# The end of a fused transformer layer: order of the last gate/up and down products, the engine of the last norms, and the last store

## The chip, the cores and the metric

The kernel runs on the 8 cores of one Trainium2 chip. Each core works alone on its own share of the tokens; no data passes between cores. A core has five engines that run at the same time, each with a queue of its own that it works off in order: TensorE (PE, matrix products into PSUM), VectorE (DVE), ScalarE (ACT), GpSimd (POOL), and SyncE (SP), which here only issues transfers. The metric is the device time of the slowest core, in microseconds.

## The reference

One layer of a diffusion transformer over 2 sequences of 8192 latent tokens of width 1024, with 256 context tokens. What matters here is its second half:

```
h     = modulate(layer_norm(x), shift, scale)
mix   = token_mixer(h, ...)           # window attention + gated spatial mixing
x_mid = layer_norm(ALPHA * x + g1 * mix, ln1_g, ln1_b)
h2    = modulate(layer_norm(x_mid), shift2, scale2)
gate, up = split(h2 @ w_ffn_in)       # 2 x 2816 columns
y     = (silu(gate) * up) @ w_ffn_out # 2816 -> 1024
out   = layer_norm(ALPHA * x_mid + g2 * y, ln2_g, ln2_b)
```

The layer norm takes mean and variance over the 1024 columns of a token, subtracts the mean, multiplies by the inverse root of variance plus epsilon, and then by a gain and adds a bias, both of 1024 columns.

## The kernel before, in words

A core has 2048 tokens: 16 tiles of 128 tokens, in four groups of four tiles. Tokens lie on the partitions in the residual stream (`xm`, 128 x 1024 in float32 for a tile) and the model's columns lie on the partitions in the inputs of the matrix products (`hT`).

The hidden width of 2816 is cut into 11 rounds of 256 hidden columns. Rounds 0 to 6 run one after the other over all tiles: gate and up products (`gu`, L1160), SiLU of the gate on ScalarE (L1175), product of the two on VectorE (L1178), down products (`dn`), and the sum into `xm` on VectorE (L1209). The last four rounds (7 to 10, called late) run tile by tile: `late_gu` makes the gate and up products of a few tiles for all four rounds, and `late_dn` the down products of one tile over all four rounds in one go, 8 matmuls of 512 columns for each half of the 1024 output columns. All 8 must wait for the products of all four rounds: the waits stand ahead of the first of them. After a tile's two halves are summed, `final` (L1212) does its layer norm and its store.

A unit of `late_gu` is one of 2 x 4 (half of a round's columns, round) and has a gate part and an up part of 8 matmuls each. For groups 0 to 2 a unit covers four tiles (512 columns a matmul); for the last group it is cut into tiles 12 and 13, and tiles 14 and 15 (256 columns a matmul).

The norm in `final`: `stat` (L486) takes statistics of each half of 512 columns on VectorE (L493), joins them into mean and variance (L496), adds epsilon (L498), and GpSimd raises the sum to the power of minus one half (L500). For tiles 0 to 11 and tile 15, VectorE then does two instructions of 1024 columns: subtract the mean and multiply by the gain (L1222), then multiply by the inverse root and add the bias (L1224). For tiles 12, 13 and 14 the work is spread: VectorE makes the negative mean times the inverse root (L516), ScalarE normalizes (L1217), VectorE multiplies by the gain (L1219), and GpSimd adds the bias (L1220). Then SyncE issues a store of 128 x 1024 (L1226).

`stat` also serves the first norm (16 tiles, the halo and the context), the norm inside the gated spatial mixing, and `residual`, which makes `x_mid` from the mixer's output and then normalizes it again for `h2`.

The order on each engine's queue isn't the program's order. Each operation is given to a planner (`Plan`) with its engine, a due time (`prio`), an estimated cost, and what it comes `after`. `arrange` plays the program through once, before it is emitted: it takes, engine by engine, the operations that could start within a small slack of the earliest one, and of these the one with the lowest due time; buffers (PSUM banks, statistics slots) are dealt out in this order too. The gate and up parts draw on PSUM banks 0 to 3 (`MU`), the down products on banks 4 to 7 (`DU`). Operations that free a bank (L1175, L1178, L1209) have a due time 150 earlier than their products. What this yields is a fixed order for each engine, and the waits between them are semaphores. Operations listed as `behind` another only keep its place in the order and wait for nothing.

The due times of the end of the program, with `base` = 950:

```
late_gu(8, 4, base + 185, 10)
late_dn(4, 4, base + 193, 20)
late_gu(12, 2, base + 285, 5)
late_dn(8, 4, base + 293, 20)
late_gu(14, 2, base + 325, 5)
late_dn(12, 4, base + 375, 10)
```

The third number is the due time of the first unit or tile and the fourth the step to the next.

Of the kernel before, what the change touches and what calls it, by code (L numbers as in the profile page):

```python
# [9 lines left out]
ALU = mybir.AluOpType  # L10
# [4 lines left out]
NT = 16  # L15
# [7 lines left out]
EPS = 1e-5  # L23
# [287 lines left out]
def build_nc():  # L311
# [169 lines left out]

    def stat(prio, srcs, n, after, eps):

        w = len(srcs)  # L486
        st = Tile([tuple(('st', i + x) for x in range(w)) for i in range(0, 12, w)])
        m = 6 * n // 512
        b = []
        for i, src in enumerate(srcs):  # L490
            def f(e, i=i, src=src):
                for h in range(n // 512):
                    ins = e.bn_stats(out=stt[:, sid(st) + i, 6 * h:6 * h + 6], in_=src()[:, 512 * h:512 * h + 512])  # L493
                return ins
            a = P.op('dve', prio, 0.68 * n / 512, f, after=after[i], takes=[st] if i == 0 else [])
            b.append(P.op('dve', prio - 40, 0.21, lambda e, i=i: e.bn_aggr(  # L496
                out=mv[:, sid(st) + i, 0:2], in_=stt[:, sid(st) + i, 0:m]), after=[a]))
        v = P.op('dve', prio - 40, 0.17, lambda e: e.tensor_scalar(  # L498
            out=mv[:, sid(st):sid(st) + w, 4], in0=mv[:, sid(st):sid(st) + w, 1], scalar1=eps, scalar2=None, op0=ALU.add), after=b)
        r = P.op('pool', prio - 40, 0.75, lambda e: e.tensor_tensor(  # L500
            out=mv[:, sid(st):sid(st) + w, 2], in0=mv[:, sid(st):sid(st) + w, 4], in1=neghalf[:, 0:w], op=ALU.pow),
            after=[v, ms_nh])
        return r, st

    def mean_of(st, i=0):
# [538 lines left out]
    def residual(g, base, step, psb, tb, ld_ln):  # L1044
        tiles = []
        for i in range(4):
            t = 4 * g + i
            prio = base + step * i - i
            xs = xm[g][:, i, :]
            ld = P.dma('sp', prio + i, 512, lambda e, xs=xs, t=t: e.dma_start(out=xs, in_=xh[(t + 1) * 128:(t + 2) * 128, :]),  # L1050
                       'xm%d' % t, after=xm_free[g])
            rs = []
            for h in range(2):
                ps = banks(*psb)

                def f(e, ps=ps, h=h, i=i):
                    for k in range(8):
                        ins = e.matmul(bank(ps), lhsT=mg[g][:, k, i * 128:(i + 1) * 128], rhs=woutb[:, k, h * 512:(h + 1) * 512],  # L1058
                                       start=(k == 0), stop=(k == 7))
                    return ins  # L1060
                mm = P.op('pe', prio + i, 1.73, f, after=[t_mg[(m, g)] for m in range(8)] + t_wo, behind=xm_free[g], takes=[ps])
                wo_done[(t, h)] = mm
                rs.append(P.op('dve', prio + i - 150, 0.75, lambda e, ps=ps, h=h, xs=xs: e.scalar_tensor_tensor(
                    out=xs[:, h * 512:(h + 1) * 512], in0=xs[:, h * 512:(h + 1) * 512], scalar=2.0 * ALPHA, in1=bank(ps),
                    op0=ALU.mult, op1=ALU.add), after=[mm, ld], gives=[ps]))
            r, st = stat(prio + i, [lambda xs=xs: xs], 1024, [rs], 4 * EPS)
            a = P.op('dve', prio + i, 1.3, lambda e, xs=xs, st=st: e.scalar_tensor_tensor(
                out=xs, in0=xs, scalar=mean_of(st), in1=ln_v[:, 0], op0=ALU.subtract, op1=ALU.mult), after=[r, ld_ln])
            b = P.op('dve', prio + i, 1.3, lambda e, xs=xs, st=st: e.scalar_tensor_tensor(
                out=xs, in0=xs, scalar=rstd_of(st), in1=ln_v[:, 1], op0=ALU.mult, op1=ALU.add), after=[a], gives=[st])  # L1070
            t_xm[t] = b
            r, st = stat(prio + i, [lambda xs=xs: xs], 1024, [[b]], EPS)
            m = minus(st, prio + i, r)
            xb = slot('xb', 0, 1)
            xbv = lambda xb=xb: V(o_xn + 2 * KB * sid(xb), BF16, 1024)
            n = P.op('act', prio + i, 1.24, lambda e, xs=xs, st=st, xbv=xbv: e.activation(
                out=xbv(), in_=xs, func=AF.Identity, scale=rstd_of(st), bias=minus_of(st)),
                after=[m, att_done], behind=[xb_last[-1]] if xb_last else [], takes=[xb], gives=[st])
            xb_last.append(n)
            tiles.append((n, xb, xbv))  # L1080
            if i % 2 == 0:
                continue
            pair = tiles[-2:]
            cut = slice(g * 512 + (i - 1) * 128, g * 512 + (i + 1) * 128)
            for c4 in range(2):
                ps = banks(*tb)

                def f(e, ps=ps, pair=pair, c4=c4):
                    b = bankb(ps)
                    for ci in range(4):  # L1090
                        c = 4 * c4 + ci
                        for x in range(2):
                            ins = e.transpose(b[:, ci * 256 + x * 128: ci * 256 + (x + 1) * 128],  # L1093
                                              pair[x][2]()[:, c * 128:(c + 1) * 128], ident)
                    return ins
                tr = P.op('pe', prio + i, 0.5, f, after=[p[0] for p in pair], takes=[ps], gives=[p[1] for p in pair])
                for ci in range(4):
                    c = 4 * c4 + ci
                    t_h2[(g, i // 2, c)] = P.op('act', prio + i, 0.57, lambda e, ps=ps, ci=ci, c=c, cut=cut: modulate_out(
                        e, 'act', hT[:, c, cut], bankb(ps)[:, ci * 256:(ci + 1) * 256], 4, 3, c, 0),  # L1100
                        after=[tr, modc_ready[(3, c)], modc_ready[(4, c)]] + [h_done[(m_, g)] for m_ in range(8)], gives=[ps])
# [109 lines left out]

    def final(t, prio):  # L1212
        xs = xm[t // 4][:, t % 4, :]
        r, st = stat(prio, [lambda: xs], 1024, [[t_acc[(t, 0)], t_acc[(t, 1)]]], EPS)
        if t in (12, 13, 14):
            mi = minus(st, prio - 40, r)
            z = P.op('act', prio, 1.24, lambda e: e.activation(  # L1217
                out=xs, in_=xs, func=AF.Identity, scale=rstd_of(st), bias=minus_of(st)), after=[mi], gives=[st])
# [1 line left out]
            b = P.op('pool', prio, 2.4, lambda e: e.tensor_tensor(out=xs, in0=xs, in1=ln_v[:, 1], op=ALU.add), after=[a])  # L1220
        else:
            a = P.op('dve', prio, 1.3, lambda e: e.scalar_tensor_tensor(  # L1222
                out=xs, in0=xs, scalar=mean_of(st), in1=ln_v[:, 0], op0=ALU.subtract, op1=ALU.mult), after=[r, ld_ln2])
            b = P.op('dve', prio, 1.3, lambda e: e.scalar_tensor_tensor(  # L1224
                out=xs, in0=xs, scalar=rstd_of(st), in1=ln_v[:, 1], op0=ALU.mult, op1=ALU.add), after=[a], gives=[st])
        P.dma('sp', prio, 512, lambda e: e.dma_start(out=out_d[t * 128:(t + 1) * 128, :], in_=xs), 'out%d' % t, after=[b])  # L1226

    for r in range(NR):
# [39 lines left out]
    late_gu(8, 4, base + 185, 10)  # L1268
    late_dn(4, 4, base + 193, 20)
    late_gu(12, 2, base + 285, 5)  # L1270
    late_dn(8, 4, base + 293, 20)
    late_gu(14, 2, base + 325, 5)
    late_dn(12, 4, base + 375, 10)

    P.arrange()
    P.emit(nc, es)
# [142 lines left out]
```

How the kernel before makes its waits and increments, by code:

```python
            def body(engine, e=e):  # L269
                for o in self.q[e]:
                    for s, n in waits[o]:
                        engine.wait_ge(sems[s], n)
                    ins = o.fn(engine)
                    if o.tick is not None:
                        ins.then_inc(sems[o.tick[0]], 16 if o.key is not None else 1)
                if e == 'sp':
                    for k, n in sorted(final.items()):
                        engine.wait_ge(sems[k], n)
```

## Time and profile before

| what | us |
|---|---|
| median of 3 runs | 981.92 |
| lowest to highest | 981.34 to 982.61 |
| the profiled execution | 983.19 |
| its span, core 4, the slowest | 981.4 |
| spans of the eight cores | 975.6 to 981.4 |
| busy in the span: TensorE / VectorE / ScalarE / GpSimd | 897.0 / 624.9 / 321.6 / 275.3 |

The span goes from a core's first to its last instruction; the time of an execution also has what lies around it, 1.8 us here. Start times in the rows are microseconds from the start of the span on core 4. Matmuls are pipelined and their ends are modelled, so a long run of them is to be read by its whole length. Shares of busy time are averages over stages that have different limits, so they are read stage by stage. The granted clock of TensorE is a share of full speed.

### The profile page before, as it was taken

Reading aid. Unit: us, or ns where it says so; the run is one execution under the profiler, and the core shown is the slowest. Engines: PE = TensorE matmul, PEld = TensorE weight load, DVE = VectorE, ACT = ScalarE, POOL = GpSimd, SP = SyncE. Lnnn points to the kernel's source line nnn. Section 1 sums busy time; section 2 is a strip of 40 time slices with the busy share of each in tenths; the row PEclk is TensorE's granted clock in tenths of the full one; section 3 lists DMA queues with packets and bytes.
Section 4 is the critical chain, followed back from the end, with each engine's and each line's share of the span. In section 5 each row is a group of like instructions: output and inputs, shape, how many; then the busy total and the mean of one; then the engine's idle time right before and its main releaser. Section 6 shows DMA issues by size and latency. Waiting matters only on the chain.

```text
span 981.4 us, 15835 instructions; the slowest of 8 cores (975.6 to 981.4 us)
## 1 busy us (share of the span) xinstructions
PE 897.0 (91%) x5589; PEld 445.7 (45%) x5589; DVE 624.9 (64%) x1130; ACT 321.6 (33%) x497; POOL 275.3 (28%) x234
## 2 busy tenths in 40 slices
PE   1299697898999999999999999999999999999992
PEld 1245444344555444444444444444444444444761
DVE  5336687756655566776687575566556674666667
ACT  1336675546877243334435101110111001111101
POOL 6024164465464223323311630210202011000004
PEclk9999798989999999999999999999999999999997
DMA  8997621449972500027322580403304020111112
GB/s 211 195 196 179 166 87 44 108 55 167 146 106 68 172 1 1 1 86 112 106 40 75 159 196 1 86 6 81 82 4 86 1 43 1 43 64 43 44 65 86
DMA packets 30236, 83.91 MB, mean 86 GB/s; under 512 B 2896, under 2 KB 3152, under 8 KB 28496
## 3 DMA queue, kind: packets, MB, share of 16 engines
q0 software_dynamic: 18064, 34.54, 23.0%
q1 hardware_dynamic: 12096, 48.37, 14.2%
q8 instruction: 46, 0.75, 0.3%
q14 instruction: 30, 0.25, 0.1%
HBM read 109.05 MB, written 8.39 MB: 120 GB/s over the span
## 4 chain that ended last, share of the span: by engine, by line
PE 84%; DMA 6%; DVE 4%; issue 2%; ACT 1%; POOL 1%; SPq 0%; DVEq 0%; POOLq 0%; ACTq 0%
PE psum L1169 31%; PE psum L1195 15%; PE psum L1007 11%; PE psum L1058 6%; PE psum L1024 6%; DMA arena<-wqk 4%; PE psum L664 3%; PE psum L720 3%; PE psum L891 2%; PE psum L927 2%; PE psum L751 2%; DMA arena<-bsbc 1%; DVE arena L493 1%; PE psum L1093 1%; ACT arena L897 1%
## 5 line engine op out<-in xcount | busy, mean ns | idle before, releaser
L1169 PE MATMUL psum<-arena 128*128 128x512 bf16 (+1 forms) x1536 | 316.0, 361 | 0.0
L1169 PEld LDWEIGHTS psum<-arena 128*128 128x128 bf16 x1536 | 150.2, 98 | 154.1
L1175 ACT ACTIVATE arena<-psum 128x512 f32<-128x512 f32 (+1 forms) x96 | 53.9, 562 | 372.3 <-PE psum L1169 372.3
L1195 PE MATMUL psum<-arena 128*128 128x512 bf16 x704 | 163.0, 379 | 0.0
L1209 DVE TENSOR_TENSOR arena<-arena,psum 128x512 f32<-128x512 f32 x224 | 140.5, 680 | 29.8 <-PE psum L1195 29.7
L1178 DVE TENSOR_TENSOR arena<-psum,arena 128x512 bf16<-128x512 f32 (+1 forms) x96 | 62.0, 646 | 127.2 <-PE psum L1169 124.8
L500 POOL TENSOR_TENSOR arena<-arena 128x1 f32<-128x1 f32 (+1 forms) x74 | 47.9, 648 | 298.5 <-DVE arena L498 290.1
L1007 PE MATMUL psum<-arena 128*128 128x512 bf16 x512 | 117.5, 379 | 0.0
L493 DVE BATCH_NORM_STATS2 arena<-arena 128x6 f32<-128x512 f32 x152 | 98.3, 684 | 12.6 <-ACT arena L761 3.2
L1195 PEld LDWEIGHTS psum<-arena 128*128 128x128 bf16 x704 | 68.6, 98 | 82.2 <-issue 1.7
L897 ACT ACTIVATE arena<-psum 128x1024 bf16<-128x1024 f32 (+1 forms) x100 | 80.5, 852 | 25.1 <-PE psum L891 24.1
L1007 PEld LDWEIGHTS psum<-arena 128*128 128x128 bf16 x512 | 48.3, 98 | 60.4 <-issue 5.6
L1014 ACT ACTIVATE arena<-psum 128x512 f32<-128x512 f32 x64 | 38.2, 597 | 83.6 <-PE psum L1007 83.2
L1024 PE MATMUL psum<-arena 128*128 128x512 bf16 x256 | 62.2, 380 | 2.4 <-DVE arena L1029 2.4
L440 POOL DMA_DIRECT2D arena<-wff x11 | 8.9, 807 | 193.7 <-PE psum L1195 186.8
L1033 POOL TENSOR_TENSOR arena<-arena 128x512 bf16<-128x512 f32 x32 | 46.1, 1442 | 59.8 <-DVE arena L1029 54.1
L1150 POOL TENSOR_TENSOR arena<-arena 128x2048 bf16<-128x2048 f32 x11 | 49.7, 4525 | 41.3 <-PE psum L1195 27.4
L570 ACT ACTIVATE arena<-psum,arena 128x256 bf16<-128x256 bf16 (+1 forms) x96 | 52.6, 620 | 26.3 <-DVE arena L476 9.6
L1029 DVE SCALAR_TENSOR_TENSOR arena<-arena,psum 128x512 f32<-128x512 f32 x64 | 42.9, 684 | 22.7 <-PE psum L1024 21.5
L1058 PE MATMUL psum<-arena 128*128 128x512 bf16 x256 | 57.2, 379 | 0.0
L906 POOL TENSOR_TENSOR arena<-arena 128x1024 bf16<-128x1024 bf16 x20 | 43.4, 2173 | 28.7 <-ACT arena L897 28.6
L664 PE MATMUL psum<-arena 128*128 128x512 bf16 (+1 forms) x176 | 45.4, 412 | 5.2 <-DVE arena L688 2.8
(97 smaller groups left out, 897.0 us busy)
## 6 DMA issues: line engine op xcount, KB each, us to landing
arena<-xh SPq DMA_DIRECT2D x34, 512.0 KB, 8.6
arena<-wada POOLq DMA_DIRECT2D x24, 512.0 KB, 17.4
arena<-wff POOLq DMA_DIRECT2D x11, 1024.0 KB, 10.3
arena<-wff SPq DMA_DIRECT2D x11, 1024.0 KB, 7.5
out<-arena SPq DMA_DIRECT2D x16, 512.0 KB, 2.6
arena<-wc POOLq DMA_DIRECT2D x8, 768.0 KB, 19.2
arena<-wout SPq DMA_DIRECT2D x8, 512.0 KB, 4.6
arena<-rope SPq DMA_DIRECT2D x4, 512.0 KB, 12.0
```

Source lines behind the costliest of these rows:

```text
L493: ins = e.bn_stats(out=stt[:, sid(st) + i, 6 * h:6 * h + 6], in_=src()[:, 512 * h:512 * h + 512])
L570: return e.activation(out=dst, in_=src, func=AF.Identity, scale=modc[:, ks, c, which:which + 1], bias=modc[:, kb, c, which:which + 1])
L664: ins = e.matmul(bank(pq)[:, 0:n], lhsT=wqk[:, m, k], rhs=rhs(k), start=(k == 0), stop=(k == 7))
L897: x = P.op('act', prio + n * 0.1, 1.03 if len(kv) == 2 else 0.62, lambda e, ptv=ptv, sp=sp, kv=kv: e.activation(out=ptv()[:, 4 * kv[0]:4 * ...
L1007: ins = e.matmul(bank(ps), lhsT=wc1[m][:, base + k], rhs=hT[:, k, g * 512:(g + 1) * 512], start=(k == 0), stop=(k == 7))
L1024: ins = e.matmul(bank(ps), lhsT=wc1[m][:, 4 * n + k], rhs=qg[g][n][:, k, :], start=(k == 0), stop=(k == 3))
L1058: ins = e.matmul(bank(ps), lhsT=mg[g][:, k, i * 128:(i + 1) * 128], rhs=woutb[:, k, h * 512:(h + 1) * 512], start=(k == 0), stop=(k == 7))
L1169: ins = e.matmul(bank(ps)[:, 0:n], lhsT=w1v[r][:, k, lo:lo + 128], rhs=h2(k), start=(k == 0), stop=(k == 7))
L1175: s = P.op('act', prio - 150, act_cost(n), lambda e: e.activation(out=sgv(), in_=bank(pg)[:, 0:n], func=AF.Silu), after=[a], takes=[sg], g ...
L1178: m = P.op('dve', prio - 150, 0.15 + 0.54 * nt / 4, lambda e: e.tensor_tensor(out=dst, in0=bank(pu)[:, 0:n], in1=sgv(), op=ALU.mult), afte ...
L1195: ins = e.matmul(bank(ps), lhsT=actv[(r, fi, t)], rhs=w2v[r][:, fi, h * 512:(h + 1) * 512], start=(n == 0), stop=(n == 2 * len(rounds) - 1))
L1209: t_acc[(t, h)] = P.op('dve', prio - 150, 0.69, lambda e, ps=ps, part=part: e.tensor_tensor(out=part, in0=part, in1=bank(ps), op=ALU.add), ...
```

## The change

Four things are changed.

- The due times at the end: the down products of tiles 8 to 11 are 8 apart and not 20; the units of tiles 14 and 15 start 6 later; the down products of tiles 12 and 13 stand at 341 and 356, and those of tiles 14 and 15 at 395 and 405.
- In `final`, no tile takes the spread norm (the condition is now an empty tuple): all 16 have their norm on VectorE. The statistics of each half come as soon as that half is summed. The subtraction waits for mean and variance (`mean_ready`) and no longer for the power on GpSimd; the scaling waits for both.
- For tile 15 the scaling is made in two halves of 512 columns, each with a store of 256 KB of its own.
- In `stat` the planner's cost for a statistics half is 0.66 and not 0.68, for all users of `stat`; in `residual` too the subtraction waits for `mean_ready`.

```diff
+    mean_ready = {}
+
+    def stat(prio, srcs, n, after, eps, halves=False):
...
+            def f(e, hs, i=i, src=src):
+                for h in hs:
                     ins = e.bn_stats(out=stt[:, sid(st) + i, 6 * h:6 * h + 6], in_=src()[:, 512 * h:512 * h + 512])
                 return ins
-            a = P.op('dve', prio, 0.68 * n / 512, f, after=after[i], takes=[st] if i == 0 else [])
+            if halves:
+                a = []
+                for h in range(2):
+                    a.append(P.op('dve', prio, 0.66, lambda e, f=f, h=h: f(e, [h]), after=[after[i][h]], behind=a,
+                                  takes=[st] if h == 0 else []))
+            else:
+                a = P.op('dve', prio, 0.66 * n / 512, lambda e, f=f: f(e, range(n // 512)), after=after[i], takes=[st] if i == 0 else [])
...
+        mean_ready[r] = b
         return r, st
...
     (residual)
-                ... scalar=mean_of(st), in1=ln_v[:, 0], op0=ALU.subtract, op1=ALU.mult), after=[r, ld_ln])
+                ... scalar=mean_of(st), in1=ln_v[:, 0], op0=ALU.subtract, op1=ALU.mult), after=[mean_ready[r], ld_ln])
-                ... scalar=rstd_of(st), in1=ln_v[:, 1], op0=ALU.mult, op1=ALU.add), after=[a], gives=[st])
+                ... scalar=rstd_of(st), in1=ln_v[:, 1], op0=ALU.mult, op1=ALU.add), after=[a, r], gives=[st])
...
     def final(t, prio):
-        r, st = stat(prio, [lambda: xs], 1024, [[t_acc[(t, 0)], t_acc[(t, 1)]]], EPS)
-        if t in (12, 13, 14):
+        r, st = stat(prio, [lambda: xs], 1024, [[t_acc[(t, 0)], t_acc[(t, 1)]]], EPS, halves=True)
+        if t in ():
...
-                ... scalar=mean_of(st), in1=ln_v[:, 0], op0=ALU.subtract, op1=ALU.mult), after=[r, ld_ln2])
+                ... scalar=mean_of(st), in1=ln_v[:, 0], op0=ALU.subtract, op1=ALU.mult), after=[mean_ready[r], ld_ln2])
+            if t == NT - 1:
+                for h in range(2):
+                    half = slice(512 * h, 512 * h + 512)
+                    b = P.op('dve', prio, 0.69, lambda e, half=half: e.scalar_tensor_tensor(
+                        out=xs[:, half], in0=xs[:, half], scalar=rstd_of(st), in1=ln_v[:, 1, half], op0=ALU.mult, op1=ALU.add),
+                        after=[a, r], gives=[st])
+                    P.dma('sp', prio, 256, lambda e, half=half: e.dma_start(out=out_d[t * 128:(t + 1) * 128, half], in_=xs[:, half]),
+                          'out%d_%d' % (t, h), after=[b])
+                return
...
-    late_dn(8, 4, base + 293, 20)
-    late_gu(14, 2, base + 325, 5)
-    late_dn(12, 4, base + 375, 10)
+    late_dn(8, 4, base + 293, 8)
+    late_gu(14, 2, base + 331, 5)
+    late_dn(12, 2, base + 341, 15)
+    late_dn(14, 2, base + 395, 10)
```

## Rows read from the trace of the kernel before

**Rows 1.** Windows: length, busy us and count by engine, PEclk, DMA share, GB/s.

```profile
100.00:330.00 230.00, 205.60 (x1960) 108.36 (x1961) 151.61 (x321) 149.19 (x216) 106.64 (x86) 0.93 0.51 100
330.00:963.80 633.80, 633.80 (x3166) 304.25 (x3164) 413.71 (x692) 132.69 (x223) 122.42 (x92) 1.00 0.24 62
```

**Rows 2.** Chain that ended last, its end: start, length, engine, line.

```profile
950.03 10.37 PE psum L1195 x48
...
969.13 2.94 POOL arena L1220
973.08 3.29 DVE arena L1222
976.47 1.28 DVE arena L1224
```

**Rows 3.** Timeline, VectorE and GpSimd around and after the last matmul.

```profile
964.55 1.22 DVE L1219 TENSOR_TENSOR arena<-arena 128x1024 f32<-128x1024 f32 x1
965.91 6.54 POOL L1220 TENSOR_TENSOR arena<-arena 128x1024 f32<-128x1024 f32 x2 [1.61 <-DVE arena L516]
967.27 2.98 DVE L1219 TENSOR_TENSOR arena<-arena 128x1024 f32<-128x1024 f32 x1 [0.30 <-ACT arena L1217]
972.93 2.34 POOL L1220 TENSOR_TENSOR arena<-arena 128x1024 f32<-128x1024 f32 x1
```

**Rows 4.** Timeline, TensorE: runs of gate/up (L1169) and down products (L1195).

```profile
915.05 7.15 PE L1169 MATMUL psum<-arena 128*128 128x256 bf16 x64
...
949.86 13.98 PE L1195 MATMUL psum<-arena 128*128 128x512 bf16 x64
```

**Rows 5.** Timeline, VectorE and GpSimd: norm of tile 8, then single instructions.

```profile
916.11 1.29 DVE L493 BATCH_NORM_STATS2 arena<-arena 128x6 f32<-128x512 f32 x2
...
917.64 0.20 DVE L496 BATCH_NORM_AGGREGATE arena<-arena 128x2 f32<-128x12 f32 x1
...
917.94 0.15 DVE L498 TENSOR_SCALAR arena<-arena 128x1 f32<-128x1 f32 x1
918.24 0.55 POOL L500 TENSOR_TENSOR arena<-arena 128x1 f32<-128x1 f32 x1 [9.97 <-DVE arena L498]
...
920.56 0.42 DVE L1178 TENSOR_TENSOR arena<-psum,arena 128x256 bf16<-128x256 f32 x1
920.90 1.28 DVE L1224 SCALAR_TENSOR_TENSOR arena<-arena 128x1024 f32<-128x1024 f32 x1
...
950.13 0.42 DVE L1178 TENSOR_TENSOR arena<-psum,arena 128x256 bf16<-128x256 f32 x1 [0.71 <-PE psum L1169]
...
957.04 0.69 DVE L1209 TENSOR_TENSOR arena<-arena,psum 128x512 f32<-128x512 f32 x1 [0.60 <-PE psum L1195]
```

**Rows 6.** Timeline, the power on GpSimd (L500) beside two kinds of VectorE instruction.

```profile
518.70 1.28 DVE L493 BATCH_NORM_STATS2 arena<-arena 128x6 f32<-128x512 f32 x2
518.93 0.55 POOL L500 TENSOR_TENSOR arena<-arena 128x1 f32<-128x1 f32 x1 [5.09 <-DVE arena L498]
...
528.24 1.28 DVE L1067 SCALAR_TENSOR_TENSOR arena<-arena 128x1024 f32<-128x1024 f32 x1
528.43 1.50 POOL L500 TENSOR_TENSOR arena<-arena 128x1 f32<-128x1 f32 x1 [3.96 <-DVE arena L498]
```

**Rows 7.** Stores of L1226, and GB/s in 40 slices of 965 to 982 us.

```profile
DMA to landing us min/median/max: 2.6/2.6/3.6
...
GB/s 0 19 0 0 0 0 0 0 0 0 0 58 386 424 366 0 0 0 0 145 424 414 251 0 0 0 299 414 424 97 0 0 376 395 434 29 0 0 0 0
```

**Rows 8.** Windows, columns as in rows 1.

```profile
150.00:160.00 10.00, 5.86 (x69) 4.15 (x70) 7.57 (x15) 5.37 (x9) 5.48 (x4) 0.66 0.00 0
...
963.90:967.20 3.30, 0.00 (x0) 0.00 (x0) 3.03 (x4) 1.90 (x2) 1.69 (x2) 1.00 0.01 2
```

**Rows 9.** Windows of L493 alone: length, VectorE busy and count, PEclk, DMA.

```profile
100.00:330.00 230.00, 16.02 (x25) 0.93 0.51 100
```

More of the change, by code:

```diff
@@ L480, in ada @@
         return ld
-    def stat(prio, srcs, n, after, eps):
+    mean_ready = {}
+    def stat(prio, srcs, n, after, eps, halves=False):
         w = len(srcs)
@@ L490, in stat @@
         for i, src in enumerate(srcs):
-            def f(e, i=i, src=src):
-                for h in range(n // 512):
+            def f(e, hs, i=i, src=src):
+                for h in hs:
                     ins = e.bn_stats(out=stt[:, sid(st) + i, 6 * h:6 * h + 6], in_=src()[:, 512 * h:512 * h + 512])
                 return ins
-            a = P.op('dve', prio, 0.68 * n / 512, f, after=after[i], takes=[st] if i == 0 else [])
+            if halves:
[5 more added lines that the diff above has]
+                a = P.op('dve', prio, 0.66 * n / 512, lambda e, f=f: f(e, range(n // 512)), after=after[i], takes=[st] if i == 0 else [])
             b.append(P.op('dve', prio - 40, 0.21, lambda e, i=i: e.bn_aggr(
@@ L1067, in residual @@
             a = P.op('dve', prio + i, 1.3, lambda e, xs=xs, st=st: e.scalar_tensor_tensor(
-                out=xs, in0=xs, scalar=mean_of(st), in1=ln_v[:, 0], op0=ALU.subtract, op1=ALU.mult), after=[r, ld_ln])
+                out=xs, in0=xs, scalar=mean_of(st), in1=ln_v[:, 0], op0=ALU.subtract, op1=ALU.mult), after=[mean_ready[r], ld_ln])
             b = P.op('dve', prio + i, 1.3, lambda e, xs=xs, st=st: e.scalar_tensor_tensor(
-                out=xs, in0=xs, scalar=rstd_of(st), in1=ln_v[:, 1], op0=ALU.mult, op1=ALU.add), after=[a], gives=[st])
+                out=xs, in0=xs, scalar=rstd_of(st), in1=ln_v[:, 1], op0=ALU.mult, op1=ALU.add), after=[a, r], gives=[st])
             t_xm[t] = b
@@ L1222, in final @@
             a = P.op('dve', prio, 1.3, lambda e: e.scalar_tensor_tensor(
-                out=xs, in0=xs, scalar=mean_of(st), in1=ln_v[:, 0], op0=ALU.subtract, op1=ALU.mult), after=[r, ld_ln2])
+                out=xs, in0=xs, scalar=mean_of(st), in1=ln_v[:, 0], op0=ALU.subtract, op1=ALU.mult), after=[mean_ready[r], ld_ln2])
+            if t == NT - 1:
[7 more added lines that the diff above has]
+                return
             b = P.op('dve', prio, 1.3, lambda e: e.scalar_tensor_tensor(
-                out=xs, in0=xs, scalar=rstd_of(st), in1=ln_v[:, 1], op0=ALU.mult, op1=ALU.add), after=[a], gives=[st])
+                out=xs, in0=xs, scalar=rstd_of(st), in1=ln_v[:, 1], op0=ALU.mult, op1=ALU.add), after=[a, r], gives=[st])
         P.dma('sp', prio, 512, lambda e: e.dma_start(out=out_d[t * 128:(t + 1) * 128, :], in_=xs), 'out%d' % t, after=[b])
```

## Prediction

> **What bounds the kernel now.** I read the table by stage first [rows 1]. Between 330 and 963.8 us TensorE is busy for all of its 633.80 us, at a granted clock of 1.00, while VectorE works 413.71 us: that stage is bound by matmuls, and the change keeps every one of them. Before 330 us nothing is full: TensorE 205.60 of 230 us, VectorE 151.61, ScalarE 149.19.
>
> Then the chain of waits, from its end [rows 2]. The last down products of tiles 12 to 15 run as one block; behind them stand GpSimd's add on L1220, VectorE's subtract on L1222 and its scaling on L1224. The tail is what the change can shorten, so I read it next, one instruction at a time [rows 3]. TensorE ends at 949.86 + 13.98 = 963.84 [rows 4], the span at 981.40: the tail is 17.56 us. Two VectorE instructions are far too long in it: L1219 takes 2.98 us where its twin takes 1.22, and L1222 takes 3.29 [rows 2] where a scale-and-shift of this size takes 1.28 [rows 5]. Both lie beside an L1220 on GpSimd [rows 3]. The second shows it best: GpSimd runs from 972.93 to 975.27, and VectorE's instruction ends 1.1 us after that, at 976.37.
>
> **The order of the matmuls.** A gate/up unit of two tiles is 16 matmuls, 7.15 / 4 = 1.79 us with its start and end, 1.73 back to back; a tile's down products are 16 of 512 columns, 3.45 us [rows 4]. The plan takes the lowest due time among what is ready. With u0 to u7 the units of tiles 12 and 13, v0 to v7 those of 14 and 15, and D8 to D15 the down products, the due times of before give u0 u1 D8, four units, D9, four units, D10, four units, D11, v6 v7, D12 D13 D14 D15; the run of 64 gate/up matmuls (four units) and the last run of 64 down matmuls (four tiles) in [rows 4] are parts of that order. The due times of the change give u0 u1 D8 u2 u3 D9 u4 D10 u5 u6 D11 u7 v0 v1 v2 D12 v3 v4 v5 D13 v6 v7 D14 D15. The sum of TensorE's work is unchanged.
>
> Three costs follow. (a) D8 to D11 now lie within 4 x 3.45 + 5 x 1.73 = 22.5 us. VectorE has about 4.4 us for each tile (two sums of 0.69, statistics 1.29, 0.20 and 0.15, two of 1.28, some gaps of 0.10) and 0.42 for each unit's product [rows 5], some 20.5 us in all. It fits, narrowly; four units behind it let VectorE catch up. I cost it at nothing: four banks of PSUM on each side cover it. Without that cover a product would wait behind one norm instruction, up to 1.28 us of TensorE.
> (b) D14 needs the product of v7, and nothing else is left for TensorE. Before, D12 and D13 stood between. VectorE starts such a product 950.13 - 949.86 = 0.27 us after the last matmul's end, takes 0.42 [rows 5], and a wait between engines costs 0.15 (917.94 + 0.15 to 918.24 [rows 5]); TensorE's refill of about 0.1 is an estimate from those gaps. That is 0.9 us of new idle time. Bounds: 0.7 if the refill is free, 2.2 if a 1.28 us norm instruction of tile 13 stands ahead of the product. I take 0.9: by the due times, tile 13's subtract starts 1.3 us before the product is ready. Such a gap should not cost clock: 963.90 to 967.20 shows 1.00 granted, the upper level of 2.4 GHz, with no matmul running, right behind the full stage [rows 8].
> (c) Only D14 and D15 remain back to back, so only two tiles of norm are open at TensorE's end, not four.
>
> **The tail.** Time S is the start of D14. A half's sum starts 0.27 us after its last matmul (949.86 + 4 x 1.727 + 0.27 = 957.04 [rows 5]), so the four sums are ready at S + 2.0, 3.7, 5.45 and 7.2; TensorE ends at S + 7.07, which I call E. An instruction that depends on the one before starts 0.10 after it (917.64 + 0.20 to 917.94), one that doesn't starts 0.08 early (920.56 + 0.42 against 920.90) [rows 5]. In the order of the due times VectorE does: tile 14's sums, its statistics in halves between them, aggregate to 5.5; sum 15a to 6.1; subtract 14 to 7.4; sum 15b to 8.0; scale 14 to 9.2; both statistics of 15 to 10.4, aggregate 10.7, epsilon beside, subtract 15 from 10.9 to 12.15.
>
> Subtract now starts before the power on GpSimd (L500), which therefore runs beside it. Beside statistics the power takes 0.55 us; beside a scale-and-shift with two operands in SBUF (528.24) it takes 1.50 and ends 0.41 after that one [rows 6]. So the scaling of tile 15 starts at 12.15 + 0.41 + 0.10 = 12.67, and not at 12.25. The Trainium skill speaks against this part of the change in the same sense: GPSIMD Engine Reference, section 8 (Key points), says that the engine shares its SBUF interfaces with VectorE and contends with VectorE instructions that have two SBUF inputs; the trace agrees, 1.50 against 0.55. If that rule did not hold here the sum would be 0.4 us less.
>
> The two halves of the last scaling: 0.69 each (the nearest row of 512 columns is the sum, 0.69; half of 1.28 would be 0.64), 12.67 to 13.36 and 13.28 to 13.97. That is E + 6.9. Bounds: 5.1 if only tile 15's own chain is left at E (0.11 + 0.69 + 0.76 + 0.31 + 1.38 + 0.52 + 1.30), 11.3 if one more tile of 4.4 us is behind. I take 6.9, since D13 has v6, v7 and the gap, 4.4 us, in front of D14.
>
> The store: from the end of L1224, 977.75, to the span's end are 3.65 us, of which 2.6 are issue to landing of 512 KB [rows 2, 7]. The bytes of such a store move at some 420 GB/s, 1.25 us [rows 7]; half of it saves at most 0.6. No row shows a 256 KB store, so the end is 3.0 to 3.65 us; I take 3.2. The first half leaves 0.6 us sooner and is not the last.
>
> ScalarE's three L1217, the three negations and GpSimd's three adds of 2.34 to 3.3 us go; VectorE gets for each of tiles 12 to 14 two instructions of 1.28 in place of one of 1.22, counted above.
>
> Sum: 17.56 - (6.9 + 3.2) - 0.9 = 6.6 us less. The profiled execution took 983.19 us with a span of 981.40; the same 6.6 off the median of 981.92 gives 975.3 us.
>
> **Everything ahead of the tail.** The planner is fed 0.66 for a statistics half in place of 0.68, and the subtracts of the residual stage wait for the aggregate, not for the power. From 330 us on TensorE has no idle time that could be won or given back [rows 1], so I cost the second at nothing; what hides it is the full TensorE. Before 330 us the order of five queues comes from the planner's times; 25 statistics halves lie between 100 and 330 us [rows 9]. An order may flip there, to either side. A row to price it: between 150 and 160 us TensorE was busy 5.86 us at a granted 0.66 (a mean of both levels, 1.2 and 2.4 GHz), so 10 us did the work of 3.9 at full clock, and lost 6.1 [rows 8].
>
> **Rivals.**
> 1. Forecast, 0.57: tail as above, early part within about 1.5 us, 973.8 to 976.8.
> 2. The early order shifts by 1.5 to 4 us, either way: 971.3 to 973.8, or 976.8 to 979.3. For: the planner is a greedy chooser, and one changed choice moves those behind it. Against: the change of cost is 0.02 us a half. 0.22.
> 3. The wait for v7's product becomes the bound: a norm instruction ahead of it, 2.2 us, and the two last tiles all later by 1.3: 976.6. 0.05.
> 4. VectorE is the bound: D8 to D13 leave it one tile behind at E, 4.4 us: 979.7. For: 20.5 of 22.5 us. Against: v0 to v2 and v3 to v5 each give 3.9 us to catch up. 0.04. This is the case in which the edit doesn't do what its words say: the norms queue on one engine instead of three.
> 5. One more stretch like 150 to 160 us: 975.3 + 6.1 = 981.4, no change. 0.06.
> 6. Slower: the changed costs reorder the attention stage so that TensorE waits in two more such stretches, 12.2 us: 987.5. It decides from 6.6 us of loss on. For: TensorE idles 24 us there at a granted 0.93 [rows 1]; against: the statistics are 16.02 of VectorE's 151.61 us there [rows 1, 9]. 0.06.
>
> **How the numbers follow.** Predicted 975.3, the likeliest case. Cases 1 to 4 lie between 971.3 and 979.7, 0.88 together; with the edges of 2 as unlikely ends I give 971.5 to 979.3. About 0.2% (2 us) can be told from no change. Cases 1 to 4 are faster by more than that, 0.88; case 5 is the same, 0.06; case 6 slower, 0.06.
>
> **What would show it.** In the profile after: no 128x1024 GpSimd add in the last 20 us and no VectorE scale-and-shift over 1.4 us; TensorE idle once, by about 0.9 us, ahead of D14, ended by VectorE's L1178 product; TensorE's end about 0.9 later against the same start; the last VectorE instruction 6.9 us after it; powers of 1.5 us beside subtracts; two last stores of 256 KB; span's end 3.2 us after the last scaling. It is wrong if the stage before 330 us ends more than 2 us elsewhere, if D14 waits over 2 us, or if VectorE still holds norms of tile 13 when D15 ends.

## The result, and the profile after

The changed kernel takes 972.04 us (median of 4 runs, 969.25 to 974.86) where the kernel before takes 982.26 beside it (4 runs, 981.34 to 984.46). The ratio is 0.9887 with an interval of 0.9868 to 0.9906: some 11 us less (the two medians alone give 10.2), where 6.6 were forecast. 0.9887 of 981.92 is 970.8 us, just below 971.5, the lower end of the range. The end of the kernel came out as predicted; the surplus was won some 750 us ahead of it.

The windows of the changed kernel's slowest core, number 6, with the columns of [rows 1]; the second stretch ends with the last matmul:

```profile
100.00:330.00 230.00, 205.03 (x1939) 109.64 (x1968) 149.99 (x319) 149.41 (x216) 108.30 (x87) 0.93 0.51 102
330.00:963.22 633.22, 629.32 (x3099) 303.47 (x3157) 418.89 (x694) 130.57 (x221) 137.76 (x92) 1.00 0.24 63
```

The second stretch is the full stage of before with one gap in it (some matmul records are missing here, 3099 of 3166, which makes the busy time look smaller than it is). The first stretch shows 0.93 here, as in [rows 1]. The other seven cores show 0.95 or 0.96 in it; before, all eight showed 0.92 to 0.94. So the surplus shows first in the granted clock, and not on this core.

The timeline of the changed kernel's end on the same core (start, length, engine, line; L1178 is the gate/up product, L1204 the down product, L1218 the sum, L495 the statistics, L508 the power, L1231 the subtraction, L1242 and L1236 the scaling):

```profile
943.12 5.40 PE L1178 MATMUL psum<-arena 128*128 128x256 bf16 x48
948.58 3.40 PE L1204 MATMUL psum<-arena 128*128 128x512 bf16 x15
...
956.15 7.07 PE L1204 MATMUL psum<-arena 128*128 128x512 bf16 x31 [0.68 <-DVE arena L1187]
...
962.26 1.27 DVE L1231 SCALAR_TENSOR_TENSOR arena<-arena 128x1024 f32<-128x1024 f32 x1
962.49 1.46 POOL L508 TENSOR_TENSOR arena<-arena 128x1 f32<-128x1 f32 x1 [6.57 <-DVE arena L506]
...
964.05 1.28 DVE L1242 SCALAR_TENSOR_TENSOR arena<-arena 128x1024 f32<-128x1024 f32 x1
965.25 1.28 DVE L495 BATCH_NORM_STATS2 arena<-arena 128x6 f32<-128x512 f32 x2
...
967.02 1.27 DVE L1231 SCALAR_TENSOR_TENSOR arena<-arena 128x1024 f32<-128x1024 f32 x1
967.25 1.45 POOL L508 TENSOR_TENSOR arena<-arena 128x1 f32<-128x1 f32 x1 [3.30 <-DVE arena L506]
968.80 1.41 DVE L1236 SCALAR_TENSOR_TENSOR arena<-arena 128x512 f32<-128x512 f32 x2 [0.51 <-POOL arena L508]
```

Three units (48 matmuls), D13, two units, a wait for VectorE's product, then D14 and D15: the order that the prediction derived from the due times. TensorE ends at 956.15 + 7.07 = 963.22, the scaling at 970.21, the span at 973.1. The tail is 9.9 us, where [rows 3, 4] gave 17.56. No add of 1024 columns on GpSimd is left in it, and the subtractions take 1.27 us where [rows 2] had 3.29.

### The profile page after: what moved, and what is told of

Its sections match the earlier page's. It is cut to its first block, busy times and chain, and to the rows that moved or that the text cites. A ratio compares the mean times of both kernels' runs of the same rounds, so it can differ in the third digit from the quotient of the medians.

```text
span 973.1 us, 15750 instructions; the slowest of 8 cores (966.4 to 973.1 us)
## 1 busy us (share of the span) xinstructions
PE 890.9 (92%) x5495; PEld 446.2 (46%) x5589; DVE 622.9 (64%) x1131; ACT 317.7 (33%) x494; POOL 284.6 (29%) x231
## 4 chain that ended last, share of the span: by engine, by line
PE 84%; DMA 6%; DVE 4%; issue 3%; ACT 2%; POOL 1%; DVEq 0%; POOLq 0%; SPq 0%; ACTq 0%
PE psum L1178 31%; PE psum L1204 15%; PE psum L1016 11%; PE psum L1033 6%; PE psum L1067 6%; DMA arena<-wqk 4%; PE psum L673 3%; PE psum L729 3%; PE psum L900 2%; PE psum L936 2%; PE psum L760 2%; DMA arena<-ctxb 1%; DVE arena L495 1%; PE psum L1102 1%; DVE arena L974 1%
## 5 line engine op out<-in xcount | busy, mean ns | idle before, releaser
L1178 PE MATMUL psum<-arena 128*128 128x512 bf16 (+1 forms) x1515 | 314.5, 361 | 1.1
L1178 PEld LDWEIGHTS psum<-arena 128*128 128x128 bf16 x1536 | 150.2, 98 | 154.5
L1204 PE MATMUL psum<-arena 128*128 128x512 bf16 x681 | 161.0, 379 | 1.9 <-DVE arena L1187 0.7
L508 POOL TENSOR_TENSOR arena<-arena 128x1 f32<-128x1 f32 (+1 forms) x74 | 70.9, 958 | 287.2 <-DVE arena L506 272.0
L1218 DVE TENSOR_TENSOR arena<-arena,psum 128x512 f32<-128x512 f32 x224 | 140.5, 679 | 18.8 <-PE psum L1204 18.6
L1016 PE MATMUL psum<-arena 128*128 128x512 bf16 x498 | 115.7, 379 | 1.4 <-issue 1.0
L495 DVE BATCH_NORM_STATS2 arena<-arena 128x6 f32<-128x512 f32 x152 | 99.7, 685 | 14.5 <-DMA arena<-xh 3.8
L1204 PEld LDWEIGHTS psum<-arena 128*128 128x128 bf16 x704 | 68.6, 98 | 82.7 <-issue 2.6
L1016 PEld LDWEIGHTS psum<-arena 128*128 128x128 bf16 x512 | 48.5, 98 | 61.6 <-issue 5.6
L1033 PE MATMUL psum<-arena 128*128 128x512 bf16 x246 | 60.5, 379 | 3.3 <-DVE arena L1038 2.4
L1042 POOL TENSOR_TENSOR arena<-arena 128x512 bf16<-128x512 f32 x32 | 40.6, 1269 | 60.9 <-DVE arena L1038 55.2
L1067 PE MATMUL psum<-arena 128*128 128x512 bf16 x248 | 57.1, 379 | 0.4
L673 PE MATMUL psum<-arena 128*128 128x512 bf16 (+1 forms) x171 | 43.7, 405 | 6.3 <-DVE arena L697 3.9
```

The source lines that it names most:

```text
L673: ins = e.matmul(bank(pq)[:, 0:n], lhsT=wqk[:, m, k], rhs=rhs(k), start=(k == 0), stop=(k == 7))
L1016: ins = e.matmul(bank(ps), lhsT=wc1[m][:, base + k], rhs=hT[:, k, g * 512:(g + 1) * 512], start=(k == 0), stop=(k == 7))
L1033: ins = e.matmul(bank(ps), lhsT=wc1[m][:, 4 * n + k], rhs=qg[g][n][:, k, :], start=(k == 0), stop=(k == 3))
L1178: ins = e.matmul(bank(ps)[:, 0:n], lhsT=w1v[r][:, k, lo:lo + 128], rhs=h2(k), start=(k == 0), stop=(k == 7))
L1204: ins = e.matmul(bank(ps), lhsT=actv[(r, fi, t)], rhs=w2v[r][:, fi, h * 512:(h + 1) * 512], start=(n == 0), stop=(n == 2 * len(rounds) - 1))
L1218: t_acc[(t, h)] = P.op('dve', prio - 150, 0.69, lambda e, ps=ps, part=part: e.tensor_tensor(out=part, in0=part, in1=bank(ps), op=ALU.add), ...
```

## The experiments

Two theories stood at the start. The first: all that happens at the end is worth the forecast 6.6 us, and the rest of the gain comes from the planner's 0.66 in place of 0.68, which gives the attention stage another order. The rival: the end itself is worth all 11 us. A second question was what another order gives back: clock, idle time, or both.

**The change cut in two, and the early half in two again.** The tail alone puts two lines of the change back; the early half alone, and each of its two edits alone, leave the rest as before.

```diff
 (tail alone)
-  a = P.op('dve', prio, 0.66 * n / 512, ...)
+  a = P.op('dve', prio, 0.68 * n / 512, ...)
 (residual)
-  ... op0=ALU.subtract, op1=ALU.mult), after=[mean_ready[r], ld_ln])
+  ... op0=ALU.subtract, op1=ALU.mult), after=[r, ld_ln])
```

> Only the end is changed (due times, norms on VectorE, halves); the planner's cost of a statistics half is 0.68 again for all users ahead of the end and the residual's subtraction waits for the power again, so the queues ahead of the last 80 us are those of before. Theory T (the end is worth 6.6 to 6.9 us as in the profile after: tail 9.9 us instead of 17.6, minus a gap of 0.9; the rest comes from the order before 330 us): 975.3 us, ratio 0.9930 to 0.9935. Rival U (the end is worth the whole gain of some 11 us, nothing comes from ahead of it): ratio 0.9887.

> Only what lies ahead of the end is changed (cost 0.66, residual's subtraction after mean and variance); the end is that of before. Theory T: the 4 us that the forecast lacked are here, ratio 0.995 to 0.997 (977 to 979 us), tail 17.6 us. Rival U: ratio 1.000.

> The only edit is the planner's cost of a statistics half, 0.66 for 0.68: no instruction is added or taken away, only the orders change. Theory T1 (the order between 100 and 330 us is what gains): the same as e2, ratio 0.995 to 0.997, and TensorE's full stage starts 3 to 4 us earlier. Rival T2 (the residual's earlier subtraction gains): ratio 1.000.

> The only edit is that the residual's subtraction waits for mean and variance and not for the power. Theory T1: TensorE is full from 330 us on, so nothing is won: ratio 0.999 to 1.001. Rival T2: ratio 0.995 to 0.997.

Ratios to the kernel before: the tail alone 0.9934 (0.9920 to 0.9947), the early half 0.9956 (0.9942 to 0.9971), the cost alone 0.9956 (0.9940 to 0.9971), the earlier subtraction in the residual stage alone 0.9997 (0.9988 to 1.0005). 0.9934 x 0.9956 = 0.9890, the whole change's 0.9887: the parts add up. The tail is worth 6.5 us of 983, the cost 4.3, the residual edit nothing.

**Where the 4.3 us lie.** For each core I summed the trace between the first v projection (L751 before, L760 after) and the first merge product (L1007, L1016): the stage's length, the time lost to the clock (each moment's 1 minus granted clock), and TensorE's idle time. Means over eight cores, in us; the two losses overlap, since idle time at the lower level counts in both:

| kernel | length | lost to the clock | idle |
|---|---|---|---|
| before | 140.9 | 14.5 | 21.9 |
| tail alone | 142.1 | 15.6 | 22.3 |
| residual edit alone | 141.9 | 14.9 | 22.6 |
| cost 0.66 alone | 137.5 | 9.6 | 21.2 |
| the change | 137.3 | 10.0 | 20.6 |

The first three rows have one order in this stage, so their scatter, 1.2 us, is the noise of the table. The stages behind it are alike in both orders: some 102.3 us to the residual stage, and 634.4 from there to TensorE's end (635.3 with the gap). Only cores 0 and 1 of the changed kernel's profile take 2.5 us more in the last of them, at a granted 0.97 between 500 and 600 us; no core of another kernel does. So the gain lies in this stage, and here it is mostly clock. One stretch shows it best. Between 188 and 212 us all 24 cores of the kernels with the old order (before, the tail alone, the residual edit alone) show a granted 0.79. This is one of them, the tail alone, core 2 (columns as in [rows 1]):

```profile
188.00:212.00 24.00, 19.00 (x136) 8.22 (x137) 19.07 (x27) 13.39 (x25) 18.87 (x13) 0.79 0.14 23
```

In the new order (the change, the early half, the cost alone) eight of 24 cores show 1.00 there, 13 show 0.93 or 0.94, and three show 0.64, one in each kernel. That one core is the slowest of its kernel in each of these profiles (980.2 us in the early half, 979.6 in the cost alone, 973.1 in the change, level with core 0), so it sets the time of that execution. The changed kernel's cores 1 and 6:

```profile
core 1: us, PE busy (x) PEld busy (x) DVE busy (x) ACT busy (x) POOL busy (x), PEclk, DMA share, GB/s
188.00:212.00 24.00, 22.10 (x214) 11.11 (x212) 15.37 (x29) 11.83 (x21) 17.08 (x14) 0.94 0.32 57
...
core 6: us, PE busy (x) PEld busy (x) DVE busy (x) ACT busy (x) POOL busy (x), PEclk, DMA share, GB/s
188.00:212.00 24.00, 19.22 (x156) 9.53 (x158) 16.48 (x29) 11.51 (x19) 14.90 (x12) 0.64 0.01 1
```

Core 1 issues 214 matmuls in that stretch and core 6 156, from one program. What stands in the stretch is the same in both orders: TensorE waits 2.8 us for a rotary-embedding product on VectorE ahead of the last q projection (L673). First the tail alone, core 4 (timeline, TensorE):

```profile
185.98 1.89 PE L673 MATMUL psum<-arena 128*128 128x512 bf16 x8
...
191.32 3.43 PE L673 MATMUL psum<-arena 128*128 128x512 bf16 x8 [2.81 <-DVE arena L697]
...
204.61 3.19 PE L729 MATMUL psum<-arena 128*128 128x512 bf16 x7 [0.34 <-issue]
```

Then the same wait in the changed kernel, in three cores: 5, 1 (two lines) and 6 (two lines).

```profile
189.02 1.89 PE L673 MATMUL psum<-arena 128*128 128x512 bf16 x8 [2.81 <-DVE arena L697]
...
187.68 3.45 PE L673 MATMUL psum<-arena 128*128 128x512 bf16 x8 [2.81 <-DVE arena L697]
199.85 1.90 PE L729 MATMUL psum<-arena 128*128 128x512 bf16 x8
...
191.22 3.57 PE L673 MATMUL psum<-arena 128*128 128x512 bf16 x8 [2.81 <-DVE arena L697]
205.99 3.60 PE L729 MATMUL psum<-arena 128*128 128x512 bf16 x8
```

Eight such matmuls take 1.89 us at the upper level of 2.4 GHz and 3.4 to 3.6 at the lower one of 1.2 GHz. In the old order all 24 cores are slow behind the wait (3.28 to 3.57 us), and core 4 is slow once more in the u projection (L729) 13 us later. In the new order core 5 stays at full speed after the same wait (1.00), core 1 is slow once (0.94), and core 6 is slow there and again at 206 us (0.64). From first v projection to first merge product core 1 takes 218.7 - 82.4 = 136.3 us, core 6 226.5 - 84.4 = 142.1. So the changed cost didn't remove the wait; it rid most cores of what followed it.

**Filling the wait.** To the tail alone, eleven matmuls of 512 columns are added ahead of that q projection, whose result nobody reads, so that TensorE works while it waits.

```diff
+    P.filler = lambda e, y: e.matmul(bank(y.takes[0])[:, 0:512], lhsT=wst[:, 0, :], rhs=..., start=True, stop=True)
+    qk_mm[-1].fill = (y[0], 11)     # y: a later operation whose PSUM bank is free by then
```

> As e1 (the end changed, the queues ahead of it as before), and TensorE gets 11 matmuls of 512 columns without use (their bank is overwritten by the next product) just ahead of the last q projection of group 3, where it stands idle for 2.8 us in every order, waiting for a rope product of VectorE. No order is changed. Theory C (what the new order gains is granted clock: 0.79 between 188 and 212 us in each of 24 cores of the old order, 0.93 to 1.00 in 21 of 24 cores of the new): with the gap filled the clock of that stretch rises to 0.9 or more, and the ratio falls from 0.9934 to 0.990 to 0.9915. Rival O (the new order gains by shorter waits, the clock only follows): the clock may rise, the ratio stays at 0.993 to 0.995.

```profile
190.62 2.54 PE L1308 MATMUL psum<-arena 128*128 128x512 bf16 x11
193.59 1.89 PE L686 MATMUL psum<-arena 128*128 128x512 bf16 x8 [0.43 <-DVE arena L710]
```

These are core 1's lines of that kernel (L1308 the useless matmuls, L686 the q projection). With them the projection starts no earlier, but it runs at full speed, 1.89 us; all eight cores show 0.93 between 188 and 212 us, in place of 0.79. The ratio to before goes from 0.9934 to 0.9911 (0.9894 to 0.9927); the stage is 138.3 us, with 10.9 lost to the clock in place of 15.6. So lost clock alone, in the old order and with work added, is worth some 2 to 4 us. (The two intervals overlap a little, and the two kernels were timed on different chips, each beside the kernel before; the mean stage says 3.8.)

**Other costs for the planner.** Is it the direction of the number that pays, or the order that happens to follow? The tail alone again, with 0.64 and with 0.70.

```diff
-  a = P.op('dve', prio, 0.68 * n / 512, ...)
+  a = P.op('dve', prio, 0.64 * n / 512, ...)      # and 0.70 in the other
```

> As e1, with the planner's cost of a statistics half at 0.64 in place of 0.68 (0.66 in the change). No instruction differs, only the orders. Theory C: the time goes with the granted clock between 150 and 230 us and with nothing else, to either side: ratio 0.984 to 0.999, and 0.990 or less only if the stretch from 188 to 212 us is above 0.9 in most cores. Rival N (0.66 gains because it is nearer to the measured 0.64 to 0.69): 0.64 gains as 0.66 does, ratio 0.988 to 0.990.

> As e11 with 0.70. Theory C: as there, either side, with the clock. Rival N: 0.70 is further from the measured time than 0.68, so nothing is gained against e1 or something lost: ratio 0.993 to 0.997.

0.64 gave 0.9930 (0.9910 to 0.9951), no gain over 0.68's 0.9934. Its order has no 2.8 us wait ahead of the last q projection either, and its mean stage is 139.7 us, 2.4 shorter than the tail alone, with 18.6 us idle; but 14.1 are lost to the clock, and its cores lie far apart (spans of 969.2 to 977.6 us), so the slowest one gains nothing. 0.70 gave 0.9878 (0.9862 to 0.9895), as much as 0.66 in the full change. A lower number isn't what pays, nor one nearer to the measured 0.64 to 0.69 us of a half. 0.70 also speaks against clock as the whole story: its stage is 135.8 us with 11.9 lost to the clock, more than the change's 10.0, and with 17.5 us idle in place of 20.6. The 2.8 us wait isn't there. Its core 1 in the same place:

```profile
183.70 1.89 PE L673 MATMUL psum<-arena 128*128 128x512 bf16 x8
185.53 0.39 PE L900 MATMUL psum<-arena 64*128 64x512 bf16 x2
185.85 0.39 PE L694 MATMUL psum<-arena 128*128 128x512 bf16 x1
186.54 0.38 PE L694 MATMUL psum<-arena 128*128 128x512 bf16 x1 [0.31 <-DVE arena L777]
```

The last q projection goes straight through; the longest wait of that kind between 180 and 213 us is then 0.83.

**The edits of the end, one at a time.** Norms, halves and their due times, without the new order of products; and the order of products alone, with the norms as before.

```diff
 (final norms alone: halves=True, if t in (), last store in halves; the due times of before)
     late_gu(12, 2, base + 285, 5); late_dn(8, 4, base + 293, 20); late_gu(14, 2, base + 325, 5)
+    late_dn(12, 2, base + 375, 10); late_dn(14, 2, base + 395, 10)
 (order alone: the due times of the change)
     if t in (12, 13, 14):      # as before
```

> Of the change only what is in final (all norms on VectorE, statistics by halves, subtraction before the power, last scaling and store in halves); due times, the cost 0.68 and the residual are those of before. By the prediction's terms: no new gap ahead of tile 14 (0.9 us saved against e1), but four tiles of 4.4 to 4.7 us of norm on VectorE against 3.45 us of down products each, so VectorE ends some 1 to 3 us later after TensorE: tail 10.5 to 13 us, ratio 0.993 to 0.9955. If the due times were what counts, the tail stays over 14 us, ratio over 0.9965.

> Of the change only the due times of the end; tiles 12 to 14 keep the norm over three engines, tile 15 its whole store. The gap of 0.85 us ahead of tile 14 is there; the adds of tiles 12 and 13 on GpSimd are done early, that of tile 14 still stands beside tile 15's subtraction: tail 12 to 15 us instead of 17.6, ratio 0.9955 to 0.9985. If the norms on VectorE are all that counts, the ratio is 1.000 or above, by the gap.

The norms alone: 0.9985 (0.9975 to 0.9994), 1.5 us. The expected tail of 10.5 to 13 us was too short, and the ratio is the one given for the case that the due times are what counts. TensorE ends at 951.61 + 13.98 = 965.59 and the span at 980.9, a tail of 15.3:

```profile
951.61 13.98 PE L1204 MATMUL psum<-arena 128*128 128x512 bf16 x64
966.47 0.68 DVE L1218 TENSOR_TENSOR arena<-arena,psum 128x512 f32<-128x512 f32 x1
971.81 1.28 DVE L1242 SCALAR_TENSOR_TENSOR arena<-arena 128x1024 f32<-128x1024 f32 x1 [0.51 <-POOL arena L508]
...
976.57 1.42 DVE L1236 SCALAR_TENSOR_TENSOR arena<-arena 128x512 f32<-128x512 f32 x2 [0.51 <-POOL arena L508]
```

Four tiles of products in 14 us bring VectorE norms faster than it works them off: the last sum comes 0.9 us after TensorE's end, with two whole norms still behind it. From the first sum at 953.61 to the last scaling's end at 977.99 are 24.4 us, 6.1 for a tile, where 4.4 to 4.7 were expected. The order alone: 0.9964 (0.9951 to 0.9977), 3.5 us, a tail of 979.6 - 966.89 = 12.7:

```profile
959.82 7.07 PE L1204 MATMUL psum<-arena 128*128 128x512 bf16 x32 [0.68 <-DVE arena L525]
...
971.20 2.33 POOL L1229 TENSOR_TENSOR arena<-arena 128x1024 f32<-128x1024 f32 x1
971.34 3.28 DVE L1231 SCALAR_TENSOR_TENSOR arena<-arena 128x1024 f32<-128x1024 f32 x1 [0.52 <-POOL arena L508]
...
974.73 1.28 DVE L1242 SCALAR_TENSOR_TENSOR arena<-arena 128x1024 f32<-128x1024 f32 x1
```

Here the long subtraction beside GpSimd's add stands again, 3.28 us as in [rows 2]. 1.5 + 3.5 is less than the 6.5 of both. By the tails, less the gap of D14, the parts are worth 2.3 and 4.0 us and both together 6.8, so they help each other by half a microsecond: with fewer tiles open, one engine suffices, and with one engine the long subtraction goes. The ratios can't tell that much apart.

**The power ahead of the last subtraction.** The changed kernel, with the subtraction waiting for the power again.

```diff
-  ... op0=ALU.subtract, op1=ALU.mult), after=[mean_ready[r], ld_ln2])
+  ... op0=ALU.subtract, op1=ALU.mult), after=[r, ld_ln2])
```

> The changed kernel, but in the last norms the subtraction waits for the power on GpSimd again. The power then runs alone, 0.55 us in place of 1.45, and the scaling follows the subtraction by 0.10 in place of 0.51. By the working of the prediction the subtraction of tile 15 then starts some 0.9 later and the scaling some 0.5 later: the tail from TensorE's end grows from 9.9 to 10.4 us. If the two instructions did not share anything, it would grow by 0.9.

```profile
955.50 7.07 PE L1204 MATMUL psum<-arena 128*128 128x512 bf16 x31 [0.68 <-DVE arena L1187]
...
967.26 0.55 POOL L508 TENSOR_TENSOR arena<-arena 128x1 f32<-128x1 f32 x1 [4.56 <-DVE arena L506]
967.91 1.28 DVE L1231 SCALAR_TENSOR_TENSOR arena<-arena 128x1024 f32<-128x1024 f32 x1 [0.80 <-POOL arena L508]
969.30 1.41 DVE L1236 SCALAR_TENSOR_TENSOR arena<-arena 128x512 f32<-128x512 f32 x2
```

TensorE ends at 962.57, the span at 973.7: a tail of 11.1 where 10.4 was expected. The power of tile 15 is short, 0.55 us, with VectorE idle beside it. Tile 14's subtraction comes later too, 0.7 us behind TensorE's end where the changed kernel has it 1.0 ahead. The early subtraction is worth 1.2 us although it makes the power nearly three times as long. (This kernel was executed once, so it has no ratio; but on all eight cores the last scaling ends 8.15 us after the last matmul, and 7.0 in the changed kernel.)

**The gap ahead of D14.** Seven of the eight matmuls of D14's first half don't need the product of v7. They are split off, and the eighth alone waits.

```diff
+  m0 = P.op('pe', prio, ..., lambda e, f=f: f(e, 0, 7), after=acts[:-1] + [t_w2[r] for r in rounds], takes=[ps])
+  mm = P.op('pe', prio, 0.22, lambda e, f=f: f(e, 7, 8), after=[m0, acts[-1]])
```

> The changed kernel, with the first half of tile 14's down products in two operations: 7 matmuls that wait for all products but the last, and the eighth, which waits for the product of v7. The gap ahead of tile 14 was 0.85 us in the trace of after and is the cost (b) of the prediction. If it is all a wait for that one product: no gap over 0.2 us, TensorE ends 0.8 us earlier after the same start of v0, and the span is 0.5 to 0.8 us shorter (VectorE's sums of tile 14 come 0.8 earlier too): ratio 0.988 against 0.9887. If the plan is filled with another wait, the gap moves to the second matmul group of tile 14.

```profile
939.56 5.40 PE L1178 MATMUL psum<-arena 128*128 128x256 bf16 x48
944.80 3.62 PE L1205 MATMUL psum<-arena 128*128 128x512 bf16 x16
948.25 3.66 PE L1178 MATMUL psum<-arena 128*128 128x256 bf16 x32
951.75 7.07 PE L1205 MATMUL psum<-arena 128*128 128x512 bf16 x32
```

The gap is gone. From the start of the 48 products ahead of D13 to TensorE's end are 958.82 - 939.56 = 19.26 us, where the changed kernel has 963.22 - 943.12 = 20.10: 0.84 less. The ratio to before, 0.9881 (0.9861 to 0.9901), can't tell 0.8 us from nothing; the trace can.

**Put together.** The change with the split and the eleven useless matmuls of above in its 2.8 us wait; the split with the cost 0.70 and the residual stage as before; and the latter with the eleven useless matmuls where it has no 2.8 us wait.

```diff
-  a = P.op('dve', prio, 0.66 * n / 512, ...)
+  a = P.op('dve', prio, 0.70 * n / 512, ...)
-  (residual) after=[mean_ready[r], ld_ln])
+  (residual) after=[r, ld_ln])
```

> The changed kernel with the split of e6 and the matmuls of e5 together: the new order still has the idle 2.8 us, behind which 18 of 24 cores show 3 to 4 us at the lower clock, and 3 cores much more (0.64 between 188 and 212 us). Theory C: these cores lose that, the slowest core is no longer 3 to 7 us behind, ratio 0.984 to 0.987. Rival O: as e6, 0.988.

> e12's order (cost 0.70) with the split of e6. In e12's trace the wait of 2.8 us ahead of the last q projection is not there, and the stage from the first v projection to the first merge takes 135.8 us as a mean of cores against 137.3 in after (idle 17.5 against 20.6, lost to the clock 12.0 against 10.0). Theory T: the terms add: 0.9878 of e12 and 0.85 us of the split give a ratio of 0.9865 to 0.9872. Rival: the orders' gains are within the scatter of the clock, ratio 0.988 or above.

> e13 with the 11 matmuls without use of e5 and e8 at the same product, where this order has no idle time. Theory C (in e5 they gained since they lay in idle time and kept the clock): here they are on the path, 11 x 0.216 = 2.4 us, and the clock there is already at the upper level, so the kernel gets slower by 1 to 2.4 us against e13, ratio 0.9880 to 0.9895. Rival (they help wherever they stand): ratio below e13's.

The first gave 0.9863 (0.9848 to 0.9878), 969.69 us; no core of it fell to 0.64 between 188 and 212 us (0.86 to 1.00), but beside the split alone, 970.45, the difference can't be told. The second gave 0.9859 (0.9843 to 0.9876), the lowest ratio of all, though not to be told from the first; against the whole change's 0.9887 the intervals overlap a little, and the two were not timed side by side. With the useless matmuls on top it is 0.9881 (0.9865 to 0.9898):

```profile
191.08 2.54 PE L1314 MATMUL psum<-arena 128*128 128x512 bf16 x11
193.46 1.89 PE L686 MATMUL psum<-arena 128*128 128x512 bf16 x8
```

They take 2.4 us from their start to the projection's, and 0.0022 x 984 = 2.2 us in the ratio, in intervals that overlap. The mean stage is only 0.6 us longer, 136.0 against 135.4, with 9.6 us lost to the clock in place of 10.9: seven of eight cores show 0.93 between 188 and 212 us, where seven showed 0.86. So the clock there was not at the upper level all along, as the expectation had it: part of what the filler took came back, but not all.

## Why the prediction missed

**What failed** is the step "Everything ahead of the tail", costed at nothing within 1.5 us. It measures 4.3 us alone, and 0.9887 / 0.9934, 4.6 us, on top of the tail. Both of its halves had been named: the residual edit is worth nothing, as argued from the full TensorE behind 330 us, and the cost could make an order flip. The prediction's own sign of being wrong, a stage ahead of 330 us that ends more than 2 us elsewhere, is there: with the cost alone the attention stage is 3.4 us shorter. What was wrong is the size of the flip. It was taken from the size of the edit, 0.02 us a half, and that says nothing: 0.64, 0.66, 0.68 and 0.70 give four orders whose stage lasts 139.7, 137.3, 142.1 and 135.8 us. It should have been priced by what the stage has to give, 24 us of TensorE's idle time and 7% of the clock [rows 1], with both signs. Rival 2 is what happened in its mechanism, and it deserved more than 0.22; 4.3 to 4.6 us lie just beyond its 1.5 to 4. The price of one bad stretch was near: 6.1 us were taken from a row, and core 6 lost 5.8 against core 1.

**What held.** The order of all products from D8 on. VectorE keeps up with D8 to D13: TensorE waits for it only ahead of D14, and no norm of tile 13 is open at the end. The gap was put at 0.9 and is 0.84 by the split. From TensorE's end to the last scaling 6.9 were predicted, and 970.21 - 963.22 = 7.0 came; from there to the span's end 3.2 against 2.9. The tail was put at 10.1 and is 9.9; less the gap, the end won 17.56 - 9.9 - 0.84 = 6.8 us by the trace and 6.5 by the runs, where 6.6 were forecast. The power beside the subtraction takes 1.45, as [rows 6] said with 1.50, and delays the scaling by 0.51.

**What held by a wrong sum** is cost (a). The terms that it lists for a tile on VectorE (two sums of 0.69, 1.29, 0.20, 0.15, two of 1.28) add up to 5.6 us; 4.4 is what they give without the two sums. With 5.6, D8 to D11 ask for some 25 us of VectorE within 22.5, so "It fits, narrowly" doesn't follow. What carried it is the other half of the sentence, the four units that let VectorE catch up. The changed kernel's core 6 shows how closely (D11, the last scaling of tile 11, the first sum of tile 12):

```profile
929.44 3.40 PE L1204 MATMUL psum<-arena 128*128 128x512 bf16 x15
938.53 1.27 DVE L1242 SCALAR_TENSOR_TENSOR arena<-arena 128x1024 f32<-128x1024 f32 x1
941.66 0.69 DVE L1218 TENSOR_TENSOR arena<-arena,psum 128x512 f32<-128x512 f32 x1 [1.30 <-PE psum L1204]
```

Tile 11's norm ends at 939.80, some 7 us after D11, and VectorE has 1.30 us to spare before D12's first sum. Rival 4, with one tile of VectorE left over at 4.4 us, was too cheap by the same 1.2 us, and by its own rows it deserved more than 0.04. The same 4.4 stands behind the short tail that was expected of the norms alone.

The rule of the Trainium skill on which the prediction drew there (GPSIMD Engine Reference, section 8, Key points: the engine contends for shared SBUF interfaces with VectorE instructions that have two SBUF inputs) agrees with these traces: 1.45 us beside the subtraction, 0.55 with VectorE idle. The runs price the overlap: it wins 1.2 us in spite of the longer power.

**What stays open.** Why one program with one order shows 1.00, 0.94 and 0.64 on different cores behind the same wait isn't settled, nor why the old order shows 0.79 on all 24. The time at which a core comes to it doesn't tell: the changed kernel's cores 6 (0.64) and 7 (1.00) end it 0.4 us apart, at 191.2 and 191.6. A last norm without GpSimd, the power on VectorE too, wasn't tried.

## What to carry to other kernels

A number that feeds a greedy planner is an edit of every stage that it plans: price it by the idle time and lost clock of those stages, on both sides, and not by the size of the number. Time such an edit apart from the one that it came with, and try its neighbours, since another value may give the same gain or more. At a kernel's end, queue products so that few tiles are open when the matmuls stop, and let a matmul that needs a late operand wait alone.

## What the runs showed of the hardware

- One wait of 2.8 us on TensorE had three sequels among the cores of one program: none (1.00 granted over 24 us), one run of eight matmuls at the lower level, 3.45 us (0.94), or lasting loss (0.64). The last cost core 6 some 5.8 us against core 1. In the old order all 24 cores showed the same 0.79.
- Matmuls that nobody needs paid where they filled that wait (0.9934 to 0.9911; on all eight cores 0.93 granted in place of 0.79, the mean stage 3.8 us shorter). Where there was no wait they brought a higher clock too (0.93 on seven of eight cores, where seven had 0.86), but no time (0.9859 to 0.9881, the mean stage 0.6 us longer).
- A VectorE subtraction of 1024 columns beside a GpSimd add of the same size takes 3.28 us in place of 1.28 and ends 1.1 us after the add; a power on one column beside it doesn't lengthen it at all (1.27), but itself takes 1.45 in place of 0.55.
